# Sparse attention: probabilities scaled in the turning product, with diagonals built by GpSimd

## The reference

```
p   = softmax(q k^T / 8  where  key <= query) 
o   = p v                                        (block heads)
o   = g0 * o_compressed + g1 * o_selected + g2 * o_window      (sparse heads)
```

## Time and profile before

| | before |
|---|---|
| median of 3 runs | 2177.55 us |
| span of the profiled execution | 2175.7 us |
| busy over the span: TensorE | 1957.0 us (90%) |
| VectorE | 1627.0 us (75%) |
| ScalarE | 983.5 us (45%) |
| GpSimd | 439.5 us (20%) |
| attention stage, 168.3 to 214.1 us: TensorE busy | 35.07 us |
| VectorE busy | 37.59 us |
| ScalarE busy | 33.65 us |
| GpSimd busy | 0.00 us |

### The profile page before, as it was taken

The page is one execution under the profiler, slowest core; times in us unless marked ns, Lnnn a source line. Parts: engine busy times, 40 slices in busy tenths (PEclk is TensorE's granted clock), DMA queues, the critical chain, the costliest instruction groups (busy, mean ns, idle before and its releaser), DMA issues. The chain is left out here.

```text
span 2175.7 us, 40379 instructions
## 1 busy us (share of the span) xinstructions
PE 1957.0 (90%) x16140; PEld 1742.6 (80%) x16140; DVE 1627.0 (75%) x2630; ACT 983.5 (45%) x1748; POOL 439.5 (20%) x238
## 2 busy tenths in 40 slices
PE   8967799979779996997888888999999999999997
PEld 4954699968559995887777867999899998888886
DVE  3757777867659887776566565499899997777776
ACT  2527343436554333334344553445455554444444
POOL 1000000000140000541000300368677771000000
PEclk9979999999789998998999888999999999999999
DMA  7671688835228882322200024576566566777775
GB/s 261 248 205 60 217 319 306 306 122 181 73 107 300 312 314 81 117 78 80 78 4 4 2 89 152 175 226 209 182 198 200 196 195 222 241 243 241 242 241 198
DMA packets 185389, 393.19 MB, mean 181 GB/s; under 512 B 14954, under 2 KB 130282, under 8 KB 173674
## 3 DMA queue, kind: packets, MB, share of 16 engines
q1 hardware_dynamic: 166770, 373.83, 50.2%
q10 hardware_dynamic: 18434, 16.79, 2.3%
HBM read 371.17 MB, written 19.40 MB: 180 GB/s over the span
## 5 line engine op out<-in xcount | busy, mean ns | idle before, releaser
L3215 POOL TENSOR_TENSOR peer_lo<-peer_u,peer_hi 128x1024 fp32r<-128x1024 f32 x117 | 298.8, 2558 | 109.5 <-ACT peer_hi L3345 109.4
L3392 PE MATMUL route_pa<-all_h_hi,peer_hi 128*128 128x256 f32 x1024 | 292.0, 285 | 7.5 <-POOL peer_lo L3215 5.7
L3393 PE MATMUL route_pa<-all_h_lo,peer_hi 128*128 128x256 f32 x1024 | 291.2, 284 | 0.0
L3394 PE MATMUL route_pa<-all_h_hi,peer_lo 128*128 128x256 f32 x1024 | 291.0, 284 | 0.0
L1403 ACT CAST peer_hi<-peer_u 128x1024 fp32r<-128x1024 f32 x126 | 132.8, 1054 | 173.0 <-PE experts_py L1386 171.6
L1630 PE MATMUL ffn_pa<-all_h_hi,ffn_u_hi 128*128 128x256 f32 x704 | 202.0, 287 | 6.1 <-DVE ffn_u_lo L1695 6.1
L3392 PEld LDWEIGHTS route_pa<-all_h_hi,peer_hi 128*128 128x128 f32 x1024 | 197.9, 193 | 9.0 <-POOL peer_lo L3215 6.9
L1382 PE MATMUL experts_py<-peer_hi,experts_c_hi 128*128 128x512 f32 x512 | 200.0, 391 | 2.9 <-DVE experts_c_lo L1443 2.9
L1631 PE MATMUL ffn_pa<-all_h_lo,ffn_u_hi 128*128 128x256 f32 x704 | 201.4, 286 | 0.0
L1632 PE MATMUL ffn_pa<-all_h_hi,ffn_u_lo 128*128 128x256 f32 x704 | 201.3, 286 | 0.0
L1383 PE MATMUL experts_py<-peer_lo,experts_c_hi 128*128 128x512 f32 x512 | 199.9, 390 | 0.0
(11 more groups left out here) (587 smaller groups left out, 5210.7 us busy)
## 6 DMA issues: line engine op xcount, KB each, us to landing
peer_u<-in_peer_v SPq DMA_DIRECT2D x128, 512.0 KB, 3.6
peer_u<-in_peer_u SPq DMA_DIRECT2D x125, 512.0 KB, 3.5
ffnw_u<-in_ffn_columns SPq DMA_DIRECT2D x44, 1024.0 KB, 7.8
ffn_ada_w<-in_ada_w SPq DMA_DIRECT2D x40, 1024.0 KB, 5.6
ffnw_v<-in_ffn_rows SPq DMA_DIRECT2D x44, 512.0 KB, 8.7
hid_kept<-peer_g ACTq DMA_DIRECT2D x128, 128.0 KB, 1.8
all_main<-hid_kept SPq DMA_DIRECT2D x128, 128.0 KB, 3.3
l1w_w<-in_diff_w_in SPq DMA_DIRECT2D x12, 1024.0 KB, 4.8
```

The costliest lines, as they stand in the source:

```text
L3215: pool.tensor_tensor(u_lo[:, i % ring, :], raw_u(i), u_hi[:, i % ring, :].bitcast(F32), ALU.subtract).then_inc(u_split, 1)
L3392: pe.matmul(out, u_hi[:, b, cols], h_hi[:, c, :], start=(c == 0), stop=False)
L3393: pe.matmul(out, u_hi[:, b, cols], h_lo[:, c, :], start=False, stop=False)
L3394: last = pe.matmul(out, u_lo[:, b, cols], h_hi[:, c, :], start=False, stop=(c == KT - 1))
```

## The change

A new tile `diag` holds, for two pairs, four 128x128 diagonal matrices: one for each of the two heads and two query tiles. GpSimd builds each by multiplying the identity by the column of factors, one factor for each partition. VectorE only makes the factors (reciprocal, and gate for the sparse pairs) and no longer touches the probabilities. The turning multiplies the unscaled probabilities, as stationary operand, by the diagonal instead of transposing them with the identity, so that the factor of each query comes in with the turning. The first chunk of 128 columns of a head belongs to the first query tile, the other two to the second (`min(c, 1)`). The semaphore `probs` gives way to two, from VectorE to GpSimd (`factor_ready`) and from GpSimd to TensorE (`diag_ready`). GpSimd also waits until the turning two pairs back has read the place in `diag` that it writes.

```diff
+        diag = st.sb("diag", [P, 2, 2, TT, P])
...
             def turn_probs(u):
-                pe.wait_ge(probs, u + 1)
+                pe.wait_ge(diag_ready, u + 1)
                 if u >= 1:
                     pe.wait_ge(pt_ready, u)
                 for half in range(2):
                     for c in range(3):
-                        last = pe.transpose(pp[:, half, c * P:(c + 1) * P], sc[:, u % ring, half, c * P:(c + 1) * P],
-                                            k["ident"][:])
+                        last = pe.matmul(pp[:, half, c * P:(c + 1) * P], sc[:, u % ring, half, c * P:(c + 1) * P],
+                                         diag[:, u % 2, half, min(c, 1), :], start=True, stop=True)
                 last.then_inc(turned, 1)
...
                 r = sm[:, b]
-                step(dve.reciprocal(r, r))
+                last = dve.reciprocal(r, r)
                 if pairs[u][3]:
+                    step(last)
                     br, h = pairs[u][3]
                     at = br * HEADS + h
-                    step(dve.tensor_tensor(r, r, gates[:, :, at:at + 2].rearrange("p t h -> p h t"), ALU.mult))
-                for t, (lo, hi) in enumerate(parts):
-                    last = dve.tensor_tensor(sc[:, b, :, lo:hi], sc[:, b, :, lo:hi],
-                                             sm[:, b, :, t:t + 1].broadcast_to([P, 2, hi - lo]), ALU.mult)
-                last.then_inc(probs, 1)
+                    last = dve.tensor_tensor(r, r, gates[:, :, at:at + 2].rearrange("p t h -> p h t"), ALU.mult)
+                last.then_inc(factor_ready, 1)
...
+        @block.gpsimd
+        def _(pool):
+            for u in range(n_pairs):
+                pool.wait_ge(factor_ready, u + 1)
+                if u >= 2:
+                    pool.wait_ge(turned, u - 1)
+                for half in range(2):
+                    for t in range(TT):
+                        last = pool.tensor_scalar(diag[:, u % 2, half, t, :], k["ident"][:],
+                                                  sm[:, u % ring, half, t:t + 1], None, ALU.mult)
+                last.then_inc(diag_ready, 1)
```

More of the change, by code:

```diff
@@ L1194, in sparse_attention @@
         po = st.ps("po", [P, 2, CW])
-        scored, masked, neg_max, exped, probs, turned, pt_ready, attended, stored, dve_done = (
-            st.sem(n) for n in ("scored", "masked", "neg_max", "exped", "probs", "turned", "pt_ready",
+        scored, masked, neg_max, exped, factor_ready, diag_ready, turned, pt_ready, attended, stored, dve_done = (
+            st.sem(n) for n in ("scored", "masked", "neg_max", "exped", "factor_ready", "diag_ready", "turned", "pt_ready",
                                 "attended", "stored", "dve_done"))
```

## The result

Slower, by more than the forecast and beyond its range: 2195.31 us median of 4 runs (2192.89 to 2197.15) against 2178.44, ratio 1.0071 [1.0058, 1.0084], some 15.5 us.

The account below looks back on a forecast made before the run. The prediction took a loop through TensorE, VectorE and now GpSimd to bound the attention stage, growing 0.62 (turning) + 0.30 (scaling moved to GpSimd) = 0.92 us. Over the stage +4.1 us: 2177.55 + 4.1 = about 2181.7 us, range 2175.5 to 2190.

Parts of the forecast that it names:

- I take 0.30, 1.20 us for the four, because the affine selection is the same shape.: GpSimd's diagonal builds in the attention stage: 0.30 us each, 1.20 a pair, priced from the affine selection of 128x128.
- The bounds, 0.20 and 0.70: GpSimd's time per diagonal build: at 0.20 us the sum is +1.7 us, at 0.70 it is +13.7.
- the clock's cost was kept at 1.7: TensorE's slow-clock stretch around the first turnings costs 1.7 us before the change and was taken to stay.
- The loop: Attention stage, turning to turning two pairs on: 6.57 us before, growing by 0.92 to between 6.7 and 7.5.
- The turning: TensorE, attention stage: twelve product instructions take 1.43 us in place of 0.81, +0.62 a pair.
- The hand-overs: Attention stage: VectorE to GpSimd takes 0.16 us, out of GpSimd 0.04.
- VectorE idle before masking: Sign that the forecast is right: in the attention stage VectorE waits for the scores before masking.
- wrong: GpSimd's mean over 0.40: Sign that the forecast is wrong: GpSimd's build instructions in the attention stage average over 0.40 us.
- GpSimd is the bound: Rival, attention stage: fetching the factor per partition makes a build 0.55 us, +10.1 us, 2187.7; chance 0.30.
- A product at four times a transpose: Rival, TensorE's turning: 2.97 us in place of 1.43, +14.9 us, 2192.4; chance 0.04.
- ScalarE binds: Rival, attention stage: ScalarE's 2.45 to 2.72 us a pair set the pace, faster, 2170.0; chance 0.04.
- The clock stays up and GpSimd is quick: Rival, attention stage: 0.25 us a build and no slow stretch, +1.2 us, 2178.8; chance 0.10.

Follow-up runs that it names:

- experiment 7: Changed kernel turned by transposes, diagonals unused, with a pair's four builds made four different GpSimd instructions (factor column at 128 and 64 columns, constant, two-tensor product): 2183.41 us, single run.
- experiment 9: Changed kernel with ten spare fp32 products ahead of the first and of the eleventh turning: 2185.77 us, ratio 1.0048; also the kernel before, profiled once more.
- experiment 2: Changed kernel with a pair's four diagonals built by one GpSimd tensor_tensor of 512 columns instead of four tensor_scalar: 2183.2 us, ratio 1.0015.
- experiment 4: Changed kernel turned by transposes with the identity again, diagonals built and waited for but unused, scaling left out: 2188.68 us, ratio 1.0040.
- experiment 3: Kernel before with the turning as an fp32 product with the identity, VectorE still scaling: 2185.32 us, ratio 1.0016.

## Why the prediction was wrong

The direction of the stage, the place and the mechanism were right; two sizes were wrong, one of them the term that the chain takes six times.

**The step that failed: "I take 0.30, 1.20 us for the four, because the affine selection is the same shape."** It was 0.603, the four 2.34. The loop passes it six times: 6 x (2.34 - 1.20) = +6.8 us. Shape alone doesn't price a GpSimd instruction: at 128x128 in fp32 the affine selection and three of the builds of experiment 7 take 0.30, 0.40, 0.53 and 0.60. The bounds, 0.20 and 0.70, held it; the choice between them was made by the row nearest in shape instead of nearest in operation. The 0.40 that the prediction worked out for a two-input product from the earlier trace rows was exact (0.402), but the kernel doesn't use that instruction.

**The second: the clock's cost was kept at 1.7.** From the turnings of the changed kernel: the first came 8.11 us after the first scores, where before's 6.08 (168.36 to 174.44), the 0.3 and GpSimd's 1.14 make 7.5 (+0.6); 0 to 2 took 9.13 against 5.9 + 1.14 = 7.04 (+2.1); 10 to 11 took 4.48 against 2.80 (+1.7). Together 4.4 us, 2.7 more than the one stretch before. The 0.6 is not the change's: it lies in the first scores at the lower clock (the first masking starts 1.60 us after them, 167.44 to 169.04, before 0.96), which the second profile of the kernel before has as well. That leaves 3.8 in the other two stretches, 2.1 above the 1.7 kept. In each of them a turning lasts longer:

```profile
175.55 2.93 PE L1227 MATMUL attn_pp<-attn_diag,attn_sc 128*128 128x128 f32 x12 [4.14 <-POOL attn_diag L1302]
...
218.17 2.42 PE L1227 MATMUL attn_pp<-attn_diag,attn_sc 128*128 128x128 f32 x12 [2.48 <-POOL attn_diag L1302]
```

Both follow TensorE's two longest idle times for GpSimd in these rows. Its idling ahead of the stretch did not "stay", as the prediction had it: it grew with GpSimd's price, from 3.18 to 4.14 us, and a second one came at the end. That the idling has a part in the low clock is shown by experiment 9: filled, both stretches were at full clock. The length of a wait alone doesn't settle it, as the first turning of experiment 2 and the eleventh of experiment 4 show:

```profile
176.24 2.93 PE L1227 MATMUL attn_pp<-attn_diag,attn_sc 128*128 128x128 f32 x12 [3.24 <-POOL attn_diag L1300]
```

```profile
214.91 0.88 PE L1227 MATMUL attn_pp<-all_ident,attn_sc 128*128 128x128 f32 x6 [3.11 <-POOL attn_diag L1302]
```

The one waits about as long as the kernel before did and is slow all the same, so the shorter builds (0.97 over the stage) shortened the first stretch and ended only the second; the other waits longer than the 2.48 us above and runs at full clock. What brings the second stretch stays open.

So the stage: 45.8 + 4.1 forecast + 6.8 + 2.7 = 59.4 us, measured 59.6. GpSimd's price by itself gives 2177.55 + 10.9 = 2188.5, still inside the range; the clock takes it out, to 2191.2. The measured 2195.31 lies 4 us above that, of the size by which the rest of the program moves between profiles; by the two ratios, 1.0071 and 1.0064, the change costs 15.5 and 14.0 us, near the stage's 13.8. The range ended at 2190: it allowed 0.65 us an instruction but not the clock on top.

**What held.** The loop: with 2.34 in place of 1.20 the prediction's sums are 6.9 + 1.14 = 8.04 and 7.5 + 1.14 = 8.64; measured 8.09 and 8.08, 8.67 and 8.65. The turning: 1.53 to the values against 1.43, and alone +0.72 a loop against +0.62 (experiment 3). The hand-overs: 0.10 and 0.05 against 0.16 and 0.04. VectorE idle before masking and TensorE waiting for GpSimd, both as listed (VectorE's idling before the reciprocal, listed too, came once, 1.8 us); and "wrong: GpSimd's mean over 0.40" was the sign that came.

**The rivals.** "GpSimd is the bound" came, with 0.60 where it had 0.55, but not for its reason: fetching the factor costs 0.07 us of it, and a real second input makes the build quicker. The prediction's 0.47 from the Trainium skill (GPSIMD Engine Reference, section 3.1: about 2.6 cycles an element as a floor of two-input work) is above the two-input product's 0.402. From 128 to 512 columns that product grows by (1.041 - 0.402)/384 = 1.66 ns a column, below the 2.17 that I estimate from the page's floor; for this product, one operand of which is broadcast, the measurement decides. "A product at four times a transpose" fell: 1.60 us against 0.87 in the earlier trace rows, 1.8 times; the Trainium skill's factor of four (TensorE: Matmul & The Clock Gate, section Terms) is not seen in this stage. "ScalarE binds" fell with the loop. "The clock stays up and GpSimd is quick" was nearest to experiment 2, clock 0.97 at 0.26 us a diagonal: it had +1.2 us, and that kernel's stage was 3.2 longer than before, its time 0.15%.

## What to carry to other kernels

Moving work off a busy engine gains only if the loop through all engines gets shorter; here VectorE lost 12 us of work and the loop grew by 2.1. Before giving GpSimd a step of such a loop, price the very operation, in the fewest instructions and away from VectorE's products of two SBUF operands. And allow for what a longer wait can do to TensorE's clock behind it: here 3.8 us in two stretches, which the length of the waits alone would not have told.

## What the runs showed of the hardware

- GpSimd, 128 partitions, fp32: a multiplication by a column of factors takes 0.60 us for 128 columns and 0.45 for 64, by a constant 0.53; a product of two tensors 0.40 for 128, 0.61 for 256, 1.04 for 512.
- Beside VectorE's product of two SBUF tensors the same GpSimd product of 256 columns takes 1.12 us instead of 0.61, and VectorE loses nothing (0.692 us, 0.686 without it).
- An fp32 product of 128x128 by 128 columns costs 1.8 times its transpose (twelve instructions in 1.60 us, six in 0.87, at full clock).
- In the one profile of it, filling TensorE's two waits moved the low clock rather than ending it: 3.5 us won at two places, 1.5 given back at a third.
